# Loading the residual ahead of the projection's weights, and releasing the modulation loads from VectorE

## The reference

```
mod = (silu(c) @ ada_w + ada_b)                 # six vectors of 1024
sh1, sc1, g1, sh2, sc2, g2 = split(mod, 6)
h = rmsnorm(x, pre) * (1 + sc1) + sh1
y = attention_output(h) @ w_o                   # the projection "wo"
x = x + g1 * rmsnorm(y, post)                   # needs x again
h = rmsnorm(x, pre2) * (1 + sc2) + sh2
x = x + g2 * rmsnorm(swiglu(h, w_in, w_out), post2)
```

## Time and profile before

| | us |
|---|---|
| median of 3 runs (range) | 3415.65 (3412.96 to 3418.82) |
| the profiled execution | 3412.96 |
| its span, first to last instruction | 3411.2 |
| around the span | 1.8 |

### The profile page before, as it was taken

The page is one execution under the profiler, slowest core; times in us unless marked ns, Lnnn a source line. Parts: engine busy times, 40 slices in busy tenths (PEclk is TensorE's granted clock), DMA queues, the critical chain, the costliest instruction groups (busy, mean ns, idle before and its releaser), DMA issues. The chain is left out here.

```text
span 3411.2 us, 40262 instructions
## 1 busy us (share of the span) xinstructions
PE 2983.9 (87%) x14295; PEld 2375.1 (70%) x14295; DVE 1640.5 (48%) x2525; ACT 1350.4 (40%) x1957; POOL 778.6 (23%) x389
## 2 busy tenths in 40 slices
PE   6999893998959989575999989899989988899994
PEld 4777672887838878363666678777767866788883
DVE  6444486333453335513333312154542125799997
ACT  3444432443234432223333321122222124799994
POOL 1111020443414434110000012222102211344441
PEclk8999996999979999787999999999999989899997
DMA  5100071333513335210000022210112132678774
GB/s 218 32 19 7 10 270 41 92 97 111 199 50 92 98 113 189 92 43 32 13 12 12 0 68 68 88 49 25 58 40 80 61 105 119 217 270 267 260 264 142
DMA packets 83483, 343.28 MB, mean 101 GB/s; under 512 B 21060, under 2 KB 27492, under 8 KB 72240
## 3 DMA queue, kind: packets, MB, share of 16 engines
q1 hardware_dynamic: 63144, 316.64, 26.5%
q0 software_dynamic: 17856, 16.85, 2.3%
q10 hardware_dynamic: 2376, 8.46, 0.7%
HBM read 375.84 MB, written 45.69 MB: 124 GB/s over the span
## 5 line engine op out<-in xcount | busy, mean ns | idle before, releaser
L2560 DVE TENSOR_TENSOR ex_g_lo<-ex_g_raw,ex_g_hi 128x1024 fp32r<-128x1024 f32 x188 | 221.0, 1217 | 1.5 <-ACT ex_g_hi L2499 1.4
L2499 ACT CAST ex_g_hi<-ex_g_raw 128x1024 fp32r<-128x1024 f32 x188 | 192.0, 1054 | 2.3 <-PE psum L2445 2.2
L617 DVE TENSOR_TENSOR ff_gated<-psum,ff_silu 128x512 f32<-128x512 f32 x44 | 30.4, 692 | 313.9 <-PE psum L490 313.9
L490 PE MATMUL psum<-ff_h_hi,ff1i_w_hi 128*128 128x512 f32 x352 | 138.1, 392 | 22.9 <-POOLq L443 22.9
L490 PE MATMUL psum<-ff_h_hi,ff0i_w_hi 128*128 128x512 f32 x352 | 138.0, 392 | 22.9 <-POOLq L443 22.9
L446 POOL TENSOR_TENSOR ff0i_w_lo<-ff0i_w_raw,ff0i_w_hi 128x1024 fp32r<-128x1024 f32 x43 | 106.3, 2471 | 211.8 <-ACT ff0i_w_hi L414 211.8
L2443 PE MATMUL psum<-ex_g_hi,ex_x_hi 128*128 128x512 f32 x376 | 151.1, 402 | 0.0
L446 POOL TENSOR_TENSOR ff1i_w_lo<-ff1i_w_raw,ff1i_w_hi 128x1024 fp32r<-128x1024 f32 x43 | 106.3, 2471 | 188.4 <-ACT ff1i_w_hi L414 188.4
L2445 PE MATMUL psum<-ex_g_hi,ex_x_lo 128*128 128x512 f32 x376 | 147.3, 392 | 0.0
L2444 PE MATMUL psum<-ex_g_lo,ex_x_hi 128*128 128x512 f32 x376 | 147.2, 391 | 0.0
L2406 POOL DMA_INDIRECT expert_sums<-ex_o,token_ids x47 | 89.8, 1911 | 225.8 <-DMA expert_sums<-ex_o,token_ids 172.5
(11 more groups left out here) (544 smaller groups left out, 8298.9 us busy)
## 6 DMA issues: line engine op xcount, KB each, us to landing
ex_g_raw<-in_w_experts_gu_dram SPq DMA_DIRECT2D x32, 2048.0 KB, 7.6
ex_d_raw<-in_w_experts_d_dram SPq DMA_DIRECT2D x32, 1024.0 KB, 9.7
ff0i_w_raw<-in_ffn_in_dram SPq DMA_DIRECT2D x44, 512.0 KB, 3.5
ff1i_w_raw<-in_ffn_in_dram SPq DMA_DIRECT2D x44, 512.0 KB, 3.5
wom_w<-in_mod_w_dram SPq DMA_DIRECT2D x8, 2048.0 KB, 8.3
ff0o_w_raw<-in_ffn_out_dram SPq DMA_DIRECT2D x16, 704.0 KB, 4.6
ff1o_w_raw<-in_ffn_out_dram SPq DMA_DIRECT2D x16, 704.0 KB, 4.1
ga_w_raw<-in_w_merge_a_dram SPq DMA_DIRECT2D x16, 512.0 KB, 3.6
```

The source lines that it names most:

```text
L490: mm = nc.tensor.matmul(chip.psum[:, 2 * u + h, :], w[:, v % 2, k * P:(k + 1) * P], (a[u] if isinstance(a, tuple) else a)[:, c * n_kc + k, ...
L2499: nc.scalar.copy(cols(g_hi, n), cols(raw.g_raw[i % 3], n)).then_inc(q["g_hi_made"], 1)
L2560: nc.vector.tensor_tensor(cols(g_lo, n), cols(raw.g_raw[i % 3], n), cols(g_hi, n).bitcast(F32), ALU.subtract).then_inc(q["g_lo_made"], 1)
```

## The change

Two edits in `LaterModulation` and `project`. The head start of `summed` is no longer given by SP before its first weight load but by DVE, at the end of `start_dve`, behind the two memsets. And the load of `x` moves from `end_sp` to `start_sp`, so that it is SP's first transfer of the projection; the wait for it stays at the end. The second edit acts in `wo` alone (the other two projections have no `load_x`); the first acts in all three.

```
@@ LaterModulation
-    def start_sp(self, sp):
-        sp.sem_inc(self.summed, KD * self.slots)
+    def start_dve(self, dve):
+        dve.sem_inc(self.summed, KD * self.slots)
@@ project
     def start_sp(sp):
-        if beside:
-            beside.start_sp(sp)
+        if load_x is not None:
+            sp.dma_start(chip.x[:], load_x).then_inc(x_in, 16)
@@
     def end_sp(sp):
         if load_x is not None:
-            sp.dma_start(chip.x[:], load_x).then_inc(x_in, 16)
             sp.wait_ge(x_in, 16)
@@ start_dve(dve) in project
         nc.vector.memset(acc[:], 0.0).then_inc(added, 1)
         nc.vector.memset(sq[1][:], 0.0).then_inc(squared, 1)
+        if beside:
+            beside.start_dve(dve)
```

## The result

The changed kernel takes 3438.72 us (median of 16 runs, 3433.56 to 3450.77). The kernel before, measured again beside it, takes 3418.35 (median of 16, 3412.96 to 3433.44). The ratio is 1.006, with a 95% interval of 1.0048 to 1.0073, so the change costs 16 to 25 us. Forecast was 3434.0, in a range of 3424.5 to 3443.

A forecast was written before the change was run, and what follows sets the result against it. The prediction took `wo` to be bound by PE. Its terms, 10.4 + 7.1 + 2.1 + 0 = 19.6 us, on the profiled 3412.96 gave 3432.6, or 3435.3 at the median's level; it said 3434.0, range 3424.5 to 3443.

The forecast's parts named there:

- `x` ahead of w0: Start of `wo`: loading `x` ahead of the first weights on SP's queue delays them and PE's first product by 10.4 us.
- The increment is given after the eighth cast: In `wo`, DVE gives the head start 0.3 us after ACT's eighth cast, not when DVE's work is done.
- Rival A: In `wo`, the increment comes only when DVE has finished the memsets: 24.2 us in total, about 3439; chance 0.12.
- The gap: In `wo`, PE waits 7.1 us between first and second tile for the second tile's weights, issued late.
- The clock: In `wo`, half clock behind PE's wait for the second tile adds 2.1 us, between 0 and 2.5.
- The feed-forward projections: In `ff0o` and `ff1o` the later increment is covered by other waits and costs 0.
- Rival D: The feed-forward projections lose their cover too, 2.5 us each on top: 24.6 us, about 3439; chance 0.07.
- Rival B: Start of `wo`: `x` doesn't hold up the first weights; 9.9 us, about 3424; chance 0.10.
- Rival C: In `wo`, both waits are covered and the kernel is not slower: SP's 0.65 us, about 3415; chance 0.04.

The follow-up runs named there:

- inc_dve: Kernel before with only the head start of `summed` moved to DVE, behind the memsets; load of `x` stays at the end: ratio 1.0023, `wo` 111.31 us.
- gap_warm: Changed kernel with 24 products that nobody reads added on PE after the first tile of `wo`: `wo` 120.85 us, ratio 1.0064.
- x_first: Kernel before with only the load of `x` moved to the front of `wo`; SP keeps the head start: ratio 1.0025, `wo` 113.55 us.
- x_on_act: Kernel before with `x` loaded first but issued on ACT's own queue; SP keeps the head start: ratio 1.0002, `wo` 106.87 us.
- inc_dve_early: Kernel before with the head start given by DVE right behind L463, ahead of the eight subtractions: ratio 1.0002, `wo` 103.84 us.

## Why the prediction was right

The side, the place and the mechanism were right, and the sum of 19.6 met a `wo` that is 19.3 us longer. That the two are so close is partly luck: `x` and the gap together were put 1.1 too high and the clock 0.75 too low, and these errors nearly cancel. By its steps:

- **`x` ahead of w0: 10.4, measured 10.0.** w0 landed 13.5 us after its issue, and 14.3 after that of `x` (423.00 + 13.5 - 422.19), the 14.3 that the rows gave. The block's first transfer went out 1.62 us after the attention's last copy, where before it was 2.03; these 0.4 us make 10.0 of the 10.4. One reading was loose: the 8.3 us of the last 2048 KB ahead of `x` are the duration of another load of the same size, for that one the trace has no landing. By the formula of the Trainium skill, "DMA: Bandwidth & Descriptors", section "Anatomy of one DMA", it would have been 12.8, an estimate, and the trace doesn't agree. The section fits it to transfers issued by GpSimd, and these were SP's, so it wasn't made for this case.
- **The increment is given after the eighth cast: 0.3 us, measured 0.23** (445.35 against 437.44 + 7.68 = 445.12). Rival A needed 450.0, the end of the second memset, and is refuted by this and by the 0.24 of inc_dve. The reasoning from `go` held, with five operations in front instead of three. The eight places that the Trainium skill, "Advanced Engine Details and Errata", section "Engine Queue Depths", gives VectorE fit both, but no run here went to a ninth.
- **The gap: 7.1, measured 6.46.** Counted from PE's first product, the forecast was w1's issue at 7.2 us, 13.1 more to the second tile's start, and 13.2 for the first tile. Measured were 7.11 (446.00 - 438.89), 12.83 (458.83 - 446.00) and 13.48 (458.83 - 6.46 - 438.89). Half of the miss is in w1's way, half in the first tile, which ran at half clock a little longer.
- **The clock: 2.1, measured 2.6 behind the gap and 0.25 at the start.** This term was too small, and above its upper bound of 2.5. I had taken the 4.2 us of the start of `wo`; behind the gap it was 5.2. gap_warm shows that it is the clock. In inc_dve the same term is 1.7 behind the gap (3.5 us of half clock) and 1.0 at the start, so 2.6 is the value of one execution.
- **The feed-forward projections: 0, measured 0.** From the first product of `ff0o` to that of `ff1i` it is 177.37 us after and 177.38 before. The cover was used and not gone. Instructions in time of the kernel after, to set beside the earlier trace rows:

```profile
860.00 0.85 SPq L113 DMA_DIRECT2D ff0m_w<-in_mod_w_dram  x2
...
866.31 0.42 DVE L138 TENSOR_SCALAR ff0m_acc<-ff0m_w,act_c 128x384 f32<-128x384 f32 x1 [3.73 <-DMA ff0m_w<-in_mod_w_dram]
...
871.88 1.38 ACT L414 CAST ff0o_w_hi<-ff0o_w_raw 128x1408 fp32r<-128x1408 f32 x1 [8.74 <-PE psum L490]
...
879.16 0.72 PE L147 MATMUL psum<-ones,ff0m_acc 128*128 128x1 f32 x6
```

  The sums start 2.3 us later against the block (866.31 less the shift of 20.0 is 846.3, before 844.00), forecast 2.8, and the chunk's cast still waits for PE. Rival D is refuted.
- **Rival B**, `x` doesn't hold up w0, is refuted by the landing of 13.5 and by x_first. That completion is not in order of issue per issuing engine, as the Trainium skill says in "DMA: Bandwidth & Descriptors", section "Queues, rings and completion order", didn't help w0 here: on one queue the 512 KB landed after the 4096 KB that were issued 0.8 us before. The rival's mechanism, sharing, appears in x_on_act, on two queues, with 3.4 us.
- **Rival C**, not slower, is refuted by the interval.
- **Not in the sum: 1.6 us** in the four products behind `wo`, at half clock. These also took 3.44 us in inc_dve_early and 1.96 in x_first and inc_dve, so they don't go with an edit; where the clock stands when PE comes back from its short wait (1.05 us) differs between these executions.

The forecast of 3434.0 lies 4.7 below the median. Most of this is the level: the sum was made on a profiled execution that is 5.4 us below the median of the 16 runs of before (3412.96 against 3418.35), and the forecast allowed 1.4 for it (3434.0 less 3412.96 and 19.6). The other 0.8 us is the difference of the medians, 20.4, less the 19.6.

## What to carry to other kernels

A transfer moved to the front of a queue is paid for by whatever is issued behind it: ask what stands there and who waits for it, and if it must start early, a queue of its own costs less (here 3.4 us instead of 10.0). A bare increment on a busy engine was given here when the waits ahead of it in its program were met, not when its work was done. So put it ahead of the first wait for another engine, not behind, and don't take it as a sign that the work in front of it is finished. And where the matrix engine waits ahead of a dense stretch, work that nobody reads, as long as the wait, can be cheaper than the half clock behind it.

## What the runs showed of the hardware that was not expected

**One kernel, two paces.** The attention's last copy starts at 421.07, 420.57, 422.07 and 420.66 us in four of the executions, and at 427.36, 428.06, 427.25 and 428.15 in four others, with the same code ahead of it. The windows of one stretch of the attention show a difference, first the kernel before, then x_first:

```profile
120.00:140.00 20.00, 17.57 (x118) 12.48 (x118) 14.64 (x76) 14.66 (x42) 4.71 (x2) 0.91 0.09 28
```

```profile
120.00:140.00 20.00, 18.06 (x87) 12.82 (x84) 11.81 (x60) 11.95 (x32) 3.04 (x2) 0.66 0.09 28
```

The same 20 us were granted 0.91 and 0.66, and 118 products against 87 went through. So PE, with many short waits, is at the lower level longer in some executions than in others; what decides it, no run here shows. This makes 6 to 7 us between two executions, as much as one of the two edits: spans of single executions may not be compared, lengths from row to row may.

**A bare increment overtakes work.** In four kernels (both edits, gap_warm, inc_dve, inc_dve_early) SP issued 0.20 to 0.24 us after the last wait ahead of the increment was met, while DVE still had 1.0 to 4.7 us of work in front of it.

**Two queues share, one queue lines up.** 4096 KB beside other transfers took 27.8 us on ACT's queue and 13.1 at the front of SP's; the 512 KB on SP's took 7.3 us beside them and 13.5 behind them. The line is not perfect: 512 KB at the front took 3.4 and 3.5 us when nothing was issued behind them before they landed (inc_dve, inc_dve_early), and 3.9 when 2048 KB followed 0.6 us later (before).
